# Projecting the first two tiles without the shift, in a two-layer diffusion-style block with a routed second block

## The chip, the cores and the metric

The kernel runs on one core of a Trainium2 chip. The metric is device time in microseconds (us), from three runs of the whole program. One more execution was recorded by the hardware profiler; every row below is from that execution.

## What is computed

The program is a chain of a two-layer block with modulation, and a second block with a recurrent group, band attention, cross attention and routed experts. Only the start of each of the two layers of the first block matters here:

```python
sc = jax.nn.silu(c)
for layer in range(DEPTH):                     # DEPTH = 2
    mod = sc @ w_mod[layer] + b_mod[layer]     # (1024) @ (1024, 6144)
    shift1, scale1, gate1, shift2, scale2, gate2 = [m[:, None, :] for m in jnp.split(mod, 6, axis=-1)]
    h = rmsnorm(x, g_attn[layer]) * (1.0 + scale1) + shift1
    o = mixer_layer(h, w_in[layer], ...)       # begins with proj = h @ w_in
    ...
```

x is 512 tokens of 1024 features, w_in is 1024 by 3078, and everything is float32. The second block also needs `softplus(-lam)` of 512 numbers, far behind.

## The kernel before

**Layout.** Features lie on partitions, so x is eight pieces `xT[:, k, :]` of 128 by 512. A projection tile is 128 output features by 512 tokens. Its precision is kept by splitting both factors into a rounded part and a rest: per k three matmuls, `w_hi*h_hi`, `w_hi*h_lo` and `w_lo*h_hi` (lines 689 to 691), 24 in a tile. ScalarE makes the rounded part of a block of weights (two tiles wide, `proj_split`, L1424) and VectorE the rest (`proj_rest`, L1921); in the same way `h_hi` (`hT_r`, L1351) is made by ScalarE out of `hn`, and `h_lo` by VectorE.

**The start.** SyncE's queue loads small rows, constants, x (2 MB), two small tensors (`forget_bias_t`, `diff_lambda`), then the first 2048 columns of w_mod, which are shift1 and scale1, in eight blocks of 1 MB (`load_first`, L416), with the first two blocks of w_in (1 MB each) after the sixth and after the eighth. TensorE turns x (L628), sums its squares over the partitions (L662), multiplies silu(c) with the eight blocks (`mod_products`, L639: four column groups of 32, a 128x512 float32 matmul in each), and turns the sums into columns (`mod_fold`, L646). VectorE adds them to `pc` (L2003), forms the gain, and `norm` makes `hn = x * gain * rs` and the rest; ScalarE adds the shift as it rounds. While the w_mod blocks arrive, VectorE also does a log-sigmoid of 128x4 numbers for the second block (L1795 to L1858) and the reciprocal of the norm's root (L1861).

**The layer loop** runs twice (`Fori`). Tiles 0 and 1 are projected as a pair, k by k, as the pieces of h arrive (`proj_pair`, banks 0 and 1); tiles 2, 3, ... follow one by one in banks 0 and 1 in turn, each after the copy out of the bank (`acc_copied`). The rotary step of tile r has one fp32 matmul of its own for r < 4 (L891), issued behind tile r+1; ScalarE copies a tile to one of two buffers `raw`, and the third copy waits until the first rotary step (L2072, L2075, L2082) is done (`rope_done`). Behind tile 3 come the first of 16 further mod products (one behind each tile) and the six forget columns (L896 to L898, 24 matmuls). At tile 12 VectorE does the forget gate's decay (`decay_sum`), at tile 13 the first scores of the attention begin (L813), whose row maxima VectorE takes (L2014).

## Time and profile before

| what | value |
|---|---|
| median of 3 runs | 2440.15 us (2438.64 to 2442.23) |
| profiled execution, span | 2438.2 us |
| TensorE busy | 2266.5 us (93%) |
| VectorE busy | 1207.9 us (50%) |
| ScalarE busy | 857.1 us (35%) |
| mean granted TensorE clock | 0.982 |

The span of the profiled execution is 2.0 us under the median of the runs. A row of the timeline gives the start, the duration, the engine and line, output<-input with its shape, and in brackets the idle time of the engine before it and what ended that. PEld is the load of weights, PE the matmul; PE rows overlap because their ends are modelled, so the time from start to start is what one costs.

### The profile page before, as it was taken

The page shows a single profiled execution, that of the slowest core. Times are in us where ns is not written, and L with a number is a line of the kernel's source. Part 1 is how long each engine was busy: PE and PEld are TensorE (multiplying, and loading weights), DVE is VectorE, ACT ScalarE, POOL GpSimd, SP SyncE. Part 2 cuts the span into 40 slices and gives each one's busy share as a digit, 9 for nine tenths or more (in the row PEclk, how much of TensorE's full clock was granted, in tenths as well). Part 3 has the DMA queues.
Part 4 walks back from the last instruction along what each step waited for, and adds up shares of the span by engine and source line. Part 5 has one row for each costly group of instructions (what it writes and reads, how often), then busy time and mean ns, then how long its engine had stood idle before and what let it go on. Part 6 is the DMA issues. An engine that isn't in the chain of part 4 may idle for free.

```text
span 2438.2 us, 31772 instructions
## 1 busy us (share of the span) xinstructions
PE 2266.5 (93%) x11324; PEld 1547.7 (63%) x11324; DVE 1207.9 (50%) x2321; ACT 857.1 (35%) x1565; POOL 80.9 (3%) x84
## 2 busy tenths in 40 slices
PE   6999899999999998999999999989989899887887
PEld 3667567888886766678888867758856333333332
DVE  6574736525525856665445455766243332323234
ACT  3234634323323254633223245464342222212123
POOL 0000000000000000000000000000000211111110
PEclk9999999999999999999999999999999999999999
DMA  7762063323333741043233322203315699999996
GB/s 272 208 201 70 8 213 98 102 80 104 104 79 100 214 137 36 19 121 87 95 104 97 110 71 86 79 27 121 121 44 240 268 390 387 422 398 399 412 400 275
DMA packets 214550, 414.34 MB, mean 170 GB/s; under 512 B 20951, under 2 KB 177249, under 8 KB 197857
## 3 DMA queue, kind: packets, MB, share of 16 engines
q1 hardware_dynamic: 200833, 398.68, 46.0%
q0 software_dynamic: 11520, 8.43, 1.1%
q10 hardware_dynamic: 2016, 4.81, 0.5%
q8 instruction: 115, 1.88, 0.3%
q14 instruction: 66, 0.54, 0.1%
HBM read 420.24 MB, written 25.17 MB: 183 GB/s over the span
## 4 chain that ended last, share of the span: by engine, by line
PE 72%; DMA 9%; DVE 8%; issue 5%; ACT 4%; SPq 1%; ACTq 0%; DVEq 0%; PEldq 0%; PEld 0%; POOLq 0%
PE bank L765 10%; PE bank L766 9%; PE bank L767 9%; DMA arena<-in_expert_up_w 8%; PE bank L689 7%; PE bank L691 6%; PE bank L690 6%; PE bank L1190 5%; PE bank L1191 2%; PE bank L1199 2%; PE bank L813 2%; PE bank L790 2%; DVE tmp L1789 1%; PE bank L639 1%; PE bank L803 1%
## 5 line engine op out<-in xcount | busy, mean ns | idle before, releaser
L1190 PE MATMUL bank<-arena,xT 128*64 128x512 f32 x560 | 265.6, 631 | 49.9 <-DMA arena<-in_expert_up_w 37.8
L689 PE MATMUL bank<-hT_r,arena_r 128*128 128x512 f32 x704 | 286.2, 407 | 10.4 <-DVE arena_r L1980 3.0
L691 PE MATMUL bank<-hT_r,arena_r 128*128 128x512 f32 x704 | 275.4, 391 | 0.0
L767 PE MATMUL bank<-hT_r,arena_r 128*128 128x512 f32 x704 | 274.0, 389 | 0.0
L1191 PE MATMUL bank<-arena,xT 128*64 128x512 f32 x560 | 266.0, 632 | 0.0
L690 PE MATMUL bank<-arena_r 128*128 128x512 f32 x656 | 256.3, 391 | 0.0
L2410 DVE TENSOR_TENSOR hT<-hT,bank 64x512 f32<-64x512 f32 x80 | 54.9, 686 | 316.8 <-PE bank L1178 220.2
L766 PE MATMUL bank<-arena_r,S_r 128*128 128x512 f32 x528 | 205.5, 389 | 0.0
L1190 PEld LDWEIGHTS bank<-arena,xT 128*64 128x64 f32 x560 | 79.1, 145 | 172.0 <-issue 155.6
L689 PEld LDWEIGHTS bank<-hT_r,arena_r 128*128 128x128 f32 x704 | 132.4, 188 | 69.5 <-issue 20.1
L1199 PE MATMUL bank<-arena,hT 128*64 128x512 f32 x560 | 128.8, 604 | 25.6 <-ACT hT L1731 25.2
L691 PEld LDWEIGHTS bank<-hT_r,arena_r 128*128 128x128 f32 x704 | 132.4, 188 | 28.8
L767 PEld LDWEIGHTS bank<-hT_r,arena_r 128*128 128x128 f32 x704 | 132.1, 188 | 27.5
L690 PEld LDWEIGHTS bank<-arena_r 128*128 128x128 f32 x656 | 123.7, 189 | 25.5 <-issue 2.2
L765 PE MATMUL bank<-hT_r,S_r 128*128 128x512 f32 x352 | 138.1, 392 | 1.7 <-DVE arena_r L1789 1.7
L1727 ACT ACTIVATE hT<-bank 64x512 f32<-64x512 f32 x80 | 47.2, 591 | 262.7 <-PE bank L1191 261.8
L767 PE MATMUL bank<-arena_r 128*128 128x512 f32 x352 | 136.9, 389 | 0.0
L2129 DVE TENSOR_SCALAR tmp<-gpad,pc 128x512 f32<-128x512 f32 x44 | 24.1, 547 | 182.1 <-ACT gpad L1530 182.1
L766 PEld LDWEIGHTS bank<-arena_r,S_r 128*128 128x128 f32 x528 | 99.1, 188 | 20.0
L1934 DVE TENSOR_TENSOR arena_r<-arena,S_r 128x1024 fp32r<-128x1024 f32 x66 | 78.0, 1221 | 66.3 <-ACT S_r L1411 66.3
L1191 PEld LDWEIGHTS bank<-arena,xT 128*64 128x64 f32 x560 | 79.1, 145 | 43.8 <-issue 43.8
L766 PE MATMUL bank<-arena_r,tmp_r 128*128 128x512 f32 x272 | 105.8, 389 | 0.0
(449 smaller groups left out, 4336.4 us busy)
## 6 DMA issues: line engine op xcount, KB each, us to landing
arena<-in_expert_gate_w SPq DMA_DIRECT2D x32, 2048.0 KB, 14.8
arena<-in_expert_up_w SPq DMA_DIRECT2D x32, 2048.0 KB, 20.1
arena<-in_expert_down_w SPq DMA_DIRECT2D x32, 2048.0 KB, 20.4
arena<-in_w_up SPq DMA_DIRECT2D x88, 512.0 KB, 5.0
arena<-in_w_in SPq DMA_DIRECT2D x68, 512.0 KB, 6.0
arena<-in_w_mod SPq DMA_DIRECT2D x32, 1024.0 KB, 6.8
arena<-in_w_down SPq DMA_DIRECT2D x40, 512.0 KB, 4.0
S<-in_w_mod SPq DMA_DIRECT2D x16, 1024.0 KB, 4.9
```

Of the source, the lines that this page charges most:

```text
L689: mm(b[:, :], w_h, hT_r[:, k, :], start=start, stop=False)
L690: mm(b[:, :], w_h, lo, start=False, stop=False)
L691: return mm(b[:, :], w_l, hT_r[:, k, :], start=False, stop=stop)
L765: mm(b[:, :], w_h, hi, start=start, stop=False)
L766: mm(b[:, :], w_h, lo, start=False, stop=False)
L767: return mm(b[:, :], w_slot(arena_r, i, piece)[:, at:at + P], hi, start=False, stop=stop)
L790: ins = nc.tensor.transpose(bank[4 + tile % 2][:, kb * P:(kb + 1) * P], probs(u)[:, kb * P:(kb + 1) * P], ident)
L1190: mm(bank[half][gate0:gate0 + SUB, :], x, expert_weights(slot, 0)[:, k, :], start=k == 0, stop=k == KD - 1)
L1191: ins = mm(bank[half][up0:up0 + SUB, :], x, expert_weights(slot, 1)[:, k, :], start=k == 0, stop=k == KD - 1)
L1199: ins = mm(bank[2 + half][c * SUB:(c + 1) * SUB, :], x, expert_weights(slot, 2)[:, k, c * T:(c + 1) * T], start=k == 0, stop=k == 3)
L1934: vec.tensor_tensor(w_slot(arena_r, i, piece), w_slot(arena, i, piece), w_hi[i % 2][piece], ALU.subtract).then_inc(s["lo_ready"], 1)
L2410: tt(ea[at, :], eg[at, :], bank[half][at, :], ALU.mult).then_inc(s["act_e"], 1)
```

## The change

w_mod's first block is cut in half: the scale half of each of the eight blocks (0.5 MB each) is loaded first, right behind x and the first block of w_in, and the shift half after it. The two small tensors move to ScalarE's queue. The first two tiles are projected from `hn` without the shift, ahead of the loop (`first_pair`); the eight shift products stand between the pair's steps k = 2 to 5, then 32 small matmuls (two columns wide) multiply the same weights with the shift, and the result goes as a bias into the two copies. Then the loop makes h again, with the shift. Tiles 2 and 3 become a pair (banks 6 and 7) in both layers. In the sum of squares VectorE adds six of the eight pieces, so that TensorE has three matmuls for it and not eight. The log-sigmoid goes from the start into the loop's first pass, behind tile 11 on VectorE. Seven matmuls on constants are added while x arrives.

```diff
+            load_in(0, 0, w_in)
+            for k in (0, 1, 2, 3, 4, 5, 7):
+                load_scale(k)
+            sp.wait_ge(s["rows_turned"], 4)
+            load_scale(6)
             for k in range(KD):
-                if k == FIRST_IN:
-                    load_in(0, 0, w_in)
-                load_first(k)
+                load_shift(k)
             load_in(0, 1, w_in)
...
-            norm(0)
             pe.wait_ge(s["silu_c"], 1)
-            pe.wait_ge(s["x_updated"], KD)
             for k in range(KD):
-                pe.wait_ge(s[f"mod_in{k}"], 16)
-                mod_products(bank[0], first_w[:, k, :, :], k)
-            mod_fold(1, toep[:, 0, :], bank[6])
+                if k == 6:
+                    norm_summed(0)
+                pe.wait_ge(s[f"mod_in{4 + k // 2}"], 32)
+                first_products(bank[0], first_w[k][:, 2:4, :], k)
+            first_fold(1, toep[:, 0, :], KD)
             keep_busy(bank[5], 3, QUARTER)
+            def first_pair():
+                pe.wait_ge(s["lo_ready"], 2)
+                for k in range(KD):
+                    pe.wait_ge(s["h_ready"], k + 1)
+                    pe.wait_ge(s["h_lo_ready"], k + 1)
+                    for j in range(2):
+                        ins = proj_mm(bank[j], 0, k, j, normed_lo(k), k == 0, k == KD - 1)
+                        if k == KD - 1 and j == 0:
+                            ins.then_inc(s["tiles_done"], 1)
+                    if 2 <= k < 6:
+                        for n in (2 * k - 4, 2 * k - 3):
+                            pe.wait_ge(s[f"mod_in{n // 2}"], 32)
+                            first_products(bank[3], first_w[n][:, 0:2, :], n)
+                    if k == 6:
+                        first_fold(2, toep[:, 1, :], 0)
+                pe.wait_ge(s["shift_split"], 1)
+                for j in range(2):
+                    for k in range(KD):
+                        at = (k % 4) * QUARTER + j * P
+                        for part, w in enumerate((proj_hi(0, k // 4), proj_lo(arena_r, 0, k // 4))):
+                            ins = mm(bank[6][:, 2 * KD + 2 * j:2 * KD + 2 * j + 2], w[:, at:at + P], shift_parts[:, k, :], start=k == 0 and part == 0, stop=k == KD - 1 and part == 1)
+                ins.then_inc(s["tiles_done"], 1)
...
                         if h == 0:
-                            proj_pair(i, normed_lo, arrived)
-                        elif h >= 2:
+                            with pe.If(l > 0):
+                                proj_pair(i, normed_lo, arrived)
+                        elif h == 1:
+                            pe.wait_ge(s["lo_ready"], pieces(l, 2))
+                            pe.wait_ge(s["bias_ready"], 1)
+                            proj_pair(1, normed_lo, arrived, 6)
+                        elif h >= 4:
...
+            proj_rest(0, 1)
+            dve.wait_ge(s["tiles_done"], TILES + 2)
+            link(vec.tensor_reduce(first_bias[:, :], bank[6][:, 2 * KD:2 * KD + 4].rearrange("p (j m) -> p j m", j=2), AX.X, ALU.add))
+            vec.tensor_scalar(first_bias[:, :], first_bias[:, :], -(HD // 2) ** -0.5, None, ALU.mult).then_inc(s["bias_ready"], 1)
...
+                    if h == TERMS_AT + 1:
+                        with dve.If(l < 1):
+                            log_sigmoid_terms(pc2[:, E_LAM:E_LAM + CT], ..., link_terms)
+                            log_sigmoid_sum(pc2[:, E_LAM:E_LAM + CT], ..., link_terms)
```

SyncE's queue at the start, before (first fence) and in the changed kernel (second). `in_w_mod` 128x2048 is a whole block, 128x1024 a half; `in_w_in` x2 is one block of the projection's weights.

```order
L405 DMA hT<-in_x 128x4x1024
L406 DMA fb<-in_forget_bias_t 6x2
L407 DMA lamp<-in_diff_lambda 128x256
L416 DMA arena<-in_w_mod 128x2048 x6
L449 DMA arena<-in_w_in 128x4x256 x2
L416 DMA arena<-in_w_mod 128x2048 x2
L449 DMA arena<-in_w_in 128x4x256 x2
```

```order
L410 DMA hT<-in_x 128x4x1024
L456 DMA arena<-in_w_in 128x4x256 x2
L419 DMA arena<-in_w_mod 128x1024 x7
L419 DMA S<-in_w_mod 128x1024
L423 DMA arena<-in_w_mod 128x1024 x6
L423 DMA S<-in_w_mod 128x1024
L423 DMA arena<-in_w_mod 128x1024
L456 DMA arena<-in_w_in 128x4x256 x2
```

The first block of w_in now stands ahead of all of w_mod, and the scale halves ahead of the shift halves.

VectorE at tile 11 of the loop, before (first) and in the changed kernel (second). `rs<-rs,std 6x512` is the first step of the decay sum, `arena_r<-arena,arena_r` the rest of a block of weights.

```order
L2082 TENSOR_TENSOR arena<-tmp 128x512
L1920 REGISTER_ALU
L1921 TENSOR_TENSOR arena_r<-arena,arena_r 128x1024
L1920 REGISTER_ALU
L1921 TENSOR_TENSOR arena_r<-arena,arena_r 128x1024
L2029 ISA
L2030 TENSOR_TENSOR pc<-pc,bank 128x16
```

```order
L2191 TENSOR_TENSOR arena<-tmp 128x512
L2199 COMPARE_AND_BRANCH
L1882 TENSOR_SCALAR small<-small 128x4
L1883 RECIPROCAL small<-small 128x4
L1884 TENSOR_TENSOR small<-small 128x4
L1885 TENSOR_TENSOR small<-small 128x4
L1886 TENSOR_SCALAR small<-small 128x4
L1869 SCALAR_TENSOR_TENSOR small<-small 128x4 x7
L1893 TENSOR_SCALAR small<-pc 128x4
L1869 SCALAR_TENSOR_TENSOR small<-small 128x4
L2203 TENSOR_SCALAR pc<-small 128x4
L2204 TENSOR_SCALAR pc<-small 128x4
```

The log-sigmoid now stands between the last rotary step and the rest of block 7, ahead of the decay sum.

TensorE at the end of the pair in the changed kernel (the small matmuls are new and have no counterpart before):

```order
L873 MATMUL bank<-kc,toep 128x4
L704 MATMUL bank<-hT_r,arena_r 128x512 [waits h_lo_ready,h_ready]
L705 MATMUL bank<-arena_r 128x512
L706 MATMUL bank<-hT_r,arena_r 128x512
L704 MATMUL bank<-hT_r,arena_r 128x512
L705 MATMUL bank<-arena_r 128x512
L706 MATMUL bank<-hT_r,arena_r 128x512
L906 MATMUL bank<-shift_parts,arena_r 128x2 [waits shift_split]
L906 MATMUL bank<-shift_parts,arena_r 128x2 x31
```

The 32 small matmuls stand behind the last step of the pair and wait for the shift.

## Rows read from the trace of the kernel before

**Rows 1.** The page: busy time and share of the span.
```profile
PE 2266.5 (93%) x11324; PEld 1547.7 (63%) x11324; DVE 1207.9 (50%) x2321; ACT 857.1 (35%) x1565; POOL 80.9 (3%) x84
```

**Rows 2.** Timeline of the start: start us, us, engine, line, what.
```profile
11.53 7.28 PE L628 MATMUL bank<-kc,hT 128*128 128x128 f32 x32 [4.50 <-DMA hT<-in_x]
...
18.64 7.60 PE L662 MATMUL bank<-tmp,kc 128*128 128x512 f32 x16
...
26.16 5.36 PE L639 MATMUL bank<-arena,rt 128*32 128x512 f32 x48
...
26.37 0.69 ACT L1345 ACTIVATE std<-bank,epsc 128x512 f32<-128x512 f32 x1
...
33.49 3.35 DVE L1861 RECIPROCAL rs<-std 128x512 f32<-128x512 f32 x1
35.31 2.00 ACT L1424 ACTIVATE arena_r<-arena 128x1024 fp32r<-128x1024 f32 x2 [5.06 <-DMA arena<-in_w_in]
...
42.68 1.06 PE L646 MATMUL bank<-kc,toep 128*128 128x4 f32 x8 [0.73 <-ACT toep L1456]
...
44.67 1.42 DVE L1789 SCALAR_TENSOR_TENSOR tmp<-xT,pc,rs 128x512 f32<-128x512 f32 x2
...
47.11 0.47 PE L689 MATMUL bank<-hT_r,arena_r 128*128 128x512 f32 x1 [1.97 <-DVE arena_r L1789]
```

**Rows 3.** Windows of the same stretch: length, busy (count) by engine, clock, DMA, GB/s.
```profile
5.00:6.00 1.00, 0.00 (x0) 0.00 (x0) 0.00 (x0) 0.00 (x0) 0.00 (x0) 1.00 1.03 412
...
10.40:12.00 1.60, 0.47 (x2) 0.48 (x3) 0.00 (x0) 0.00 (x0) 0.00 (x0) 1.00 0.24 88
12.30:26.90 14.60, 14.53 (x54) 7.42 (x56) 7.29 (x19) 6.85 (x10) 0.00 (x0) 1.00 1.01 426
27.00:31.50 4.50, 4.50 (x44) 1.17 (x36) 2.11 (x14) 1.85 (x5) 0.00 (x0) 1.00 1.05 253
```

**Rows 4.** Windows by stage, same columns: the clock.
```profile
31.50:37.80 6.30, 0.02 (x4) 0.00 (x0) 5.99 (x13) 2.00 (x2) 0.00 (x0) 0.75 1.02 402
...
45.20:47.10 1.90, 0.00 (x0) 0.03 (x1) 1.67 (x4) 1.38 (x2) 0.00 (x0) 1.00 1.08 281
47.10:59.80 12.70, 12.69 (x48) 9.89 (x48) 11.72 (x17) 6.97 (x10) 0.00 (x0) 0.87 0.10 20
```

**Rows 5.** Timeline from the pair's end to the forget columns, first layer.
```profile
59.85 1.13 PE L891 MATMUL bank<-tmp,kc 128*128 128x512 f32 x2
...
61.01 0.69 DVE L2075 TENSOR_TENSOR tmp<-bank,kc 128x512 f32<-128x512 f32 x1 [0.19 <-PE bank L891]
...
73.72 1.12 PE L891 MATMUL bank<-tmp,kc 128*128 128x512 f32 x2
...
74.28 0.79 PE L896 MATMUL bank<-hT_r,wfz_r 128*6 128x512 f32 x1
```

**Rows 6.** Timeline: two matmuls of 256 columns in a row (tile 4).
```profile
82.39 0.28 PE L720 MATMUL bank<-arena_r,hT_r 128*128 128x256 f32 x1
82.51 0.28 PE L721 MATMUL bank<-arena_r 128*128 128x256 f32 x1
```

**Rows 7.** Timeline: the log-sigmoid's first and last instruction on VectorE.
```profile
30.28 0.17 DVE L1795 TENSOR_SCALAR small<-small 128x4 f32<-128x4 f32 x1 [0.27 <-ACT small L1453]
...
33.14 0.16 DVE L1858 TENSOR_SCALAR pc<-small 128x4 f32<-128x4 f32 x1
```

**Rows 8.** VectorE's timeline, tiles 11 to 13 of the first layer.
```profile
134.70 0.69 DVE L2072 TENSOR_TENSOR tmp<-tmp,kc 128x512 f32<-128x512 f32 x1 [2.44 <-ACT tmp L1479]
...
151.01 0.28 DVE L2014 CUSTOM_DVE_ANT_0 tmp<-bank,kc 128x128 f32<-128x128 f32 x1
```

**Rows 9.** Waits of TensorE's weight loads, 140 to 155 us.
```profile
PEld bank L813 <- DVE mx L2014: 2.2, 1, 2.2
```

**Rows 10.** Timeline, second layer: tile 2 begins, third rotary matmul.
```profile
761.87 0.80 PE L689 MATMUL bank<-hT_r,arena_r 128*128 128x512 f32 x1
...
775.17 1.13 PE L891 MATMUL bank<-tmp,kc 128*128 128x512 f32 x2
```

More of the change, by code:

```diff
@@ L1472, in _ @@
                     act.wait_ge(s["tiles_done"], tiles(l, h + 1))
[L1473 removed]
+                    b = bank[4 + h if h in (2, 3) else h % 2]
                     if h in ROPE:
@@ L1492, in _ @@
                         af(z6[0], bank[4][0:C_HEADS, :], ACT.Identity, bias=pc[0:C_HEADS, 106:107]).then_inc(s["z_ready"], 1)
+                    if h == TERMS_AT:
+                        with act.If(l < 1):
+                            act.wait_ge(s["lam2"], 1)
+                            af(small[:, 40:44], small[:, 40:44], ACT.Exp, scale=-1.0).then_inc(s["lam2"], 1)
                     if h == FZ_AT + 2:
@@ L1870, in sum_square @@
                     vec.tensor_tensor(rs[:, :], rs[:, :], sq[:, k % 2, :], ALU.add).then_inc(s["sq_used"], 1)
+            for k in range(KD):
+                dve.wait_ge(s["x_turned"], k + 1)
+                vec.tensor_copy(xT[:, k, :], bank[(4, 5, 1, 2)[k % 4]][:, :]).then_inc(s["x_updated"], 1)
+                if 1 <= k <= SUMMED:
+                    sum_square(0, k - 1)
+            dve.wait_ge(s["lam_exp"], 1)
+            for l in range(DEPTH):
+                lam_init = 0.8 - 0.6 * math.exp(-0.3 * l)
+                link(vec.tensor_tensor(small[:, 28:29], small[:, 21 + 2 * l:22 + 2 * l], small[:, 20 + 2 * l:21 + 2 * l], ALU.subtract))
+                link(vec.tensor_scalar(pcall[:, l, C_LAM:C_LAM + 1], small[:, 28:29], -lam_init, None, ALU.add))
+                link(vec.tensor_scalar(pcall[:, l, C_SUB:C_SUB + 1], pcall[:, l, C_SUB:C_SUB + 1], 1.0 - lam_init, None, ALU.mult))
+            link(vec.tensor_copy(pc[:, :], pcall[:, 0, :]))
             def norm_recip(n):
```

237 lines of the change are left out of this document (146 added, 91 removed).

## The prediction

> **What bounds the kernel now.** I read the page first: TensorE is busy 93% of the span [rows 1]. So over most of the program a microsecond counts only if TensorE waits for it; elsewhere it is hidden. Then the timeline of the start, because the change works there [rows 2]. TensorE runs from 11.5 to 31.5 us, idles 6.3 us until the seventh block of w_mod lands. The windows say why: the DMA engines are full all along, from 12.3 on [rows 3, 4]. So the start is bound by bytes: 8 MB of w_mod and 1 MB of w_in between x and the gain. From the last product a chain of small steps (fold at 42.68, first hn at 44.67) leads to the first projection matmul at 47.11 [rows 2]. That pair takes 12.7 us, paced by VectorE and ScalarE, and the forget columns begin at 74.28 [rows 4, 5]. I take 74.28 as the mark: behind it the program is the same up to tile 11, so what the mark moves, the end moves. Last I looked for places later in the loop where TensorE waits for VectorE, since the log-sigmoid goes there.
>
> **Part 1, the start of the first pair.** The gain now needs 1 MB of w_in and 4 MB of scale. x stops flowing at 10.4 us; then the engines are nearly idle to 12.3, where the two small tensors stand in the queue (88 GB/s) [rows 3]. These leave the queue, so I let w_in begin at 10.4. In its 1 KB packets w_in moved at 253 GB/s [rows 3]: 1.05 MB in 4.1, to 14.5. Before TensorE may sum the squares it wants six scale halves, 3.15 MB, in 4 KB packets like x, at about 404 GB/s (412 in a window of x): 7.8, to 22.3. Landing is later than flowing: 1.1 us for x (10.4 to 11.5), 3.8 for w_in (31.5 to 35.31) [rows 2, 3]; I take 1.7, nearer x since the packets are like x's: 24.0. Then two products (5.36/6 us a block of 512 columns, half of that each: 0.9) and three norm matmuls (7.60/8 each: 2.9). TensorE's clock fell to its lower level, 1.2 GHz, within the idle 6.3 us (mean 0.75), and again within the pair (mean 0.87), behind only 1.9 idle us [rows 4]. The pair's mean makes 12.7 x 0.13 x 2 = 3.3 us at half speed, a cost of 1.7. From 18.8 to 24 TensorE will be busy about a third of the time, so I expect the lower level here too, at the same 1.7. So 29.5; root 0.7 + 0.1; the reciprocal 3.35, which other work hid before and nothing hides now; 0.9 from the fold's end to the first hn (43.74 to 44.67); 2.44 from there to the first matmul [rows 2]. The pair starts at **37.0**, against 47.1: **10.1 saved**. Ends: 32.7 (w_in at 426 GB/s, 1.1 landing, clock up) and 40.8 (3.8 landing and twice the clock's price).
>
> The Trainium skill (DMA: Bandwidth & Descriptors, Specifications) puts the smallest transfer for line rate at 512 B, by which the 1 KB packets of w_in would run as fast as the blocks of w_mod. The trace disagrees, 253 against 426 GB/s [rows 3]; by the rule w_in would take 2.5 us and the start be 1.6 us earlier.
>
> **Part 2, the first pair.** Before it took 12.7 us, 48 matmuls at about 0.227 apart (10.9) with the clock low for part of it [rows 4]. Now TensorE also does eight shift products of 0.45 and a fold of 0.5 in between: 10.9 + 3.6 + 0.5 = 15.0, more than the 12.3 in which VectorE delivers, so TensorE paces it. It has idled about 5 us before, so the lower clock again: 16.7. **+4.0** (+2.3 with the clock up).
>
> **Part 3, the 32 small matmuls.** None of that size is in the trace. The nearest rows are 256-column matmuls of the same type, 0.12 apart [rows 6], and the fp32 fold with 4 columns, 1.06 us for 8 (0.13) [rows 2]. With the load of 128x128 weights in each I take 0.12: **+3.8**. Ends: 2.0, if 256 columns rather than weights set the 0.12, and 6.0, if the 0.19 of a weight load is not overlapped. By the Trainium skill (TensorE: Matmul & The Clock Gate, Part 1) the sequencer spends about 62 ns on a small matmul with hardware decode off; by that alone the 32 would take an estimated 2.0 us, and no row here shows one.
>
> **Part 4, turning round.** VectorE waits for these, reduces them and scales (0.5), enters the loop past a branch (0.5, of the 0.9 of part 1), and must make hn, h_hi and h_lo again before tiles 2 and 3 can start: 2.44 [rows 2]. **+3.5**. Nothing covers it; TensorE has no other work in the queue. Ends 3.0 and 4.5.
>
> **Part 5, tiles 2 and 3, to the mark.** Before: 14.5 us from 59.8 to 74.28 for two tiles, three rotary matmuls and one mod product. Now the pair is fed by VectorE like the first was, 12.7 with a dip of the clock after the idle 3.5 us. Rotary step 0 starts behind it, since its matmul does: its result is there 1.16 later (59.85 to 61.01), then 0.69 + 0.69 + gaps, then the third copy (0.6 + 0.1), which waited in vain for a `raw` buffer until then, then rotary matmul 2, 0.56 to the mark [rows 5]: 3.9. 16.6 against 14.5: **+2.1**.
> The mark: 37.0 + 16.7 + 3.8 + 3.5 + 12.7 + 3.9 = 77.6, **3.3 us later** than 74.3.
>
> **Part 6, the log-sigmoid.** It takes 3.0 us (30.28 to 33.30, 16 small steps) and was hidden under DMA [rows 7]. Its new place is exposed: VectorE is idle 2.44 us just before tile 11's rotary step and then does 23 instructions from 134.7 to 151.0 back to back, up to the first row maximum; and TensorE waits 2.2 us for that maximum [rows 8, 9]. The added steps stand in that chain of work, so TensorE waits 5.2: **+3.0**, in the first layer only. If it hid somewhere it would be 0.
>
> **Part 7, the second layer.** Tiles 2 and 3 as a pair save the first rotary matmul ahead of tile 2, but tile 2 starts at 761.87 because its weights' rest is ready only then, so it starts no earlier. The pair ends 10.9 later, 772.7, and rotary matmul 2 can go 3.4 behind that (part 5's chain), 776.1, against 775.17 [rows 10]: **+0.9** (0 to 1.5). Branches that skip the new blocks cost nothing visible. The sum of squares, the turning of x in four banks and the small steps on `diff_lambda` lie beside the loads; at nothing, since part 1's chain begins behind them (if x's squares were late, at most 1).
>
> Sum: -10.1 + 4.0 + 3.8 + 3.5 + 2.1 + 3.0 + 0.9 = **+7.2 us**. On the profiled span that is 2445.4; carried over to the median, 2440.15 + 7.2 = **2447.3**. A measurement of this kernel can tell about 0.2% (4.9 us) from no change.
>
> **The rivals.**
> *The clock stays up (not slower).* If TensorE keeps 2.4 GHz through the sparse products, the first pair and the second, 1.7 + 1.7 + 1.4 fall away: +2.4, 2442.5, no change. For it: the added matmuls on constants, and the clock was 1.00 in all windows up to 31.5 [rows 3]. Against it: both dips before, one of them after an idle time of only 1.9 us [rows 4]. It decides only if all three places stay up; each one alone is 1.4 to 1.7.
> *The log-sigmoid is hidden.* If TensorE's wait at tile 13 is not set by VectorE's chain, part 6 is 0 and the time 2444.3, no change. For it: the chain holds block 7's weights and the decay, for which nobody waits yet. Against: they stand ahead of the maximum in the program's order, and TensorE already waits [rows 9].
> *The scale halves land late.* With the landing of w_in (3.8 and not 1.7) and an issue that holds back, the start is 2 to 4 us later: 2450. For it: w_in's own landing [rows 2, 3]; this is also the case that the change doesn't do what it says, that scale comes hardly earlier than both did. Slower.
> *All goes well.* Start 32.7, small matmuls at 2.0 in all, the clock up: the mark is 32.7 + 15.0 + 2.0 + 3.5 + 11.3 + 3.9 = 68.4, 5.9 earlier; with +3.9 behind it the end is 2438.2, and only with the log-sigmoid hidden too, 2435.2, is it faster by over 0.2%.
>
> **How the numbers follow.** Forecast as summed 0.45; clock up 0.17; log-sigmoid hidden 0.15; late scale 0.13; all well 0.10. Slower by over 0.2%: 0.45 + 0.13 = 0.58. Within: 0.32. Faster: 0.10, the last case with whatever else I overlooked on that side. The range reaches from just under no change (2439.5, which leaves out most of the last case) to the late scale with a dear set of small matmuls (2451.5).
>
> **What would show it.** In the changed profile: the start of the first pair (37.0 against 47.1), the 32 small matmuls' length (3.8), the idle time between them and tile 2 (3.5), the forget columns' start (77.6), TensorE's wait for the first row maximum in the first layer (5.2 against 2.2 in the second), the clock in 20 to 60 us. It is wrong in size if the pair starts before 34 or after 40, and wrong in sign if the mark is before 70.

## The result, and the profile after

| kernel | median, us | ratio to before | 95% interval |
|---|---|---|---|
| before | 2440.96 (8 runs) | | |
| changed | 2454.32 (8 runs) | 1.0052 | 1.0042 to 1.0063 |

The change makes the kernel slower, by about 13 us. The forecast was 7.2 us slower, 2447.3, with a range that ended at 2451.5. So the direction was right, the size was short by some 6 us, and the measured time lies 2.8 us outside the range. The rows of the changed kernel below come from a later recording of it (e0 of the experiments, span 2452.2 us), because the one recorded first, one of the 8, ran at a low clock throughout (mean 0.84) and took 2626.4 us.

The page of the changed kernel (line 1, busy time, and TensorE's clock in 40 slices) shows the same work by the same engines as [rows 1]; TensorE is busy 15 us longer, and the clock is lower in the first slice:

```profile
span 2452.2 us, 32084 instructions
...
PE 2281.8 (93%) x11424; PEld 1559.6 (64%) x11424; DVE 1222.3 (50%) x2348; ACT 862.1 (35%) x1574; POOL 80.7 (3%) x84
...
PEclk8999999999999999999999999999999999999999
```

The timeline of its start, TensorE and what it waits for, answers to [rows 2]: norm, reciprocal, first hn, first pair (its first matmul at 36.13), the 32 small matmuls, the bias on VectorE, h made again, second pair (first matmul at 61.67), and the first forget column, which is the mark.

```profile
30.23 3.35 DVE L2081 RECIPROCAL rs<-std 128x512 f32<-128x512 f32 x1 [5.21 <-ACT std L1517]
...
33.85 1.42 DVE L1869 SCALAR_TENSOR_TENSOR tmp<-xT,pc,rs 128x512 f32<-128x512 f32 x2
...
36.13 0.52 PE L704 MATMUL bank<-hT_r,arena_r 128*128 128x512 f32 x1 [3.14 <-DVE arena_r L2090]
...
54.17 4.34 PE L906 MATMUL bank<-shift_parts,arena_r 128*128 128x2 f32 x32
58.55 0.16 DVE L2105 TENSOR_REDUCE first_bias<-bank 128x2 f32<-128x4 f32 x1 [2.87 <-PE bank L906]
...
61.67 0.76 PE L704 MATMUL bank<-hT_r,arena_r 128*128 128x512 f32 x1 [3.16 <-DVE arena_r L1869]
...
78.99 0.80 PE L953 MATMUL bank<-hT_r,wfz_r 128*6 128x512 f32 x1
```

The windows of the same stretches (after the bounds and the length: busy time of TensorE, its weight loads, VectorE, ScalarE, GpSimd; TensorE's clock; DMA share; GB/s) answer to [rows 4]. The lower level, 1.2 GHz (0.50), begins at about 57, before the small matmuls end (58.5), and lasts into the first half of the second pair:

```profile
36.10:54.20 18.10, 18.07 (x118) 12.14 (x118) 10.03 (x17) 5.96 (x9) 0.00 (x0) 0.91 0.62 209
54.20:57.00 2.80, 2.80 (x27) 2.80 (x25) 1.47 (x2) 0.00 (x0) 0.00 (x0) 0.98 1.07 146
57.00:67.00 10.00, 6.84 (x21) 5.62 (x21) 7.56 (x13) 4.87 (x7) 0.00 (x0) 0.50 0.96 266
67.00:79.00 12.00, 11.63 (x52) 7.84 (x50) 8.06 (x13) 5.92 (x9) 0.00 (x0) 0.99 0.19 73
79.00:154.00 75.00, 75.00 (x452) 55.00 (x454) 56.61 (x88) 17.34 (x24) 0.00 (x0) 1.00 0.71 211
154.00:163.00 9.00, 4.81 (x21) 3.05 (x21) 7.16 (x24) 4.03 (x11) 0.00 (x0) 0.81 0.69 234
```

The last row is the place of the log-sigmoid's cost. The waits of 140 to 170 us (engine and line, who ended the wait: total, times, longest) answer to [rows 9], where the same wait of the weight load was 2.2:

```profile
PEld bank L828 <- DVE mx L2119: 5.1, 1, 5.1
PE bank L828 <- DVE mx L2119: 4.2, 1, 4.2
```

Both rows are one wait, that of the weight load and that of the matmul behind it; the second is the time that TensorE's matmuls stand still. In the kernel before that was 1.25 us:

```profile
151.58 0.49 PE L813 MATMUL bank<-arena 32*128 32x128 f32 x4 [1.25 <-DVE mx L2014]
```

**Where the 13 us are.** I took the start of every matmul in the trace of before and in those of the experiments, lined the sequences up, and read the difference at landmarks. Minus is earlier than in the first trace of before; the numbers are us. The two last columns are kernels of the experiments below.

| place (time of before) | before again (e8) | changed (e0) | log-sigmoid back (e1) | log-sigmoid alone (e2) |
|---|---|---|---|---|
| mark, 74.3 | +0.9 | +4.7 | +4.7 | +0.8 |
| first row maximum's wait over, 151.6 | +0.9 | +7.6 | +4.7 | +3.7 |
| nine us on, 160.5 | +0.9 | +9.2 | +4.7 | +6.2 |
| end of the first attention, 280.7 | +1.1 | +11.0 | +4.7 | +6.3 |
| forget columns of layer 2, 780.1 | +0.9 | +12.1 | +5.8 | +5.9 |
| ahead of the cross attention, 1765.1 | +0.7 | +11.4 | +3.9 | +9.4 |
| behind it, 1811.1 | +0.7 | +14.5 | +7.0 | +10.7 |
| behind the first experts, 1990.7 | -2.6 | +14.9 | +7.3 | +10.1 |
| end of the experts, 2421.0 | -3.4 | +14.9 | +7.3 | +10.2 |

So in e0 about 4 to 5 us are lost at the start, 3 in the wait at tile 13, 1.6 right behind that wait, 1.8 in the first attention (where e1 loses none), 1 in layer 2 and 3 in the cross attention. The column of e8 shows how far two executions of one program lie apart: 1 us at the mark, 4 in the experts. A term below that can't be read from one trace. So the 1.8 us of the first attention say nothing of the change: e3 below, which has only tiles 2 and 3 as a pair, loses 1.9 us there in its trace, and e7 0.2.

### The profile page after: what moved, and what is told of

Same layout as the page of the kernel before. It is cut to its first block, busy times and chain, and to the rows that moved or that the text cites. A ratio compares the mean times of both kernels' runs of the same rounds, so it can differ in the third digit from the quotient of the medians.

```text
span 2624.6 us, 32084 instructions
## 1 busy us (share of the span) xinstructions
PE 2496.0 (95%) x11424; PEld 1599.0 (61%) x11424; DVE 1223.4 (47%) x2348; ACT 862.3 (33%) x1574; POOL 81.0 (3%) x84
## 4 chain that ended last, share of the span: by engine, by line
PE 82%; DVE 6%; issue 5%; ACT 4%; DMA 3%; SPq 0%; DVEq 0%; ACTq 0%; POOLq 0%
PE bank L780 10%; PE bank L781 10%; PE bank L782 10%; PE bank L704 7%; PE bank L705 6%; PE bank L706 6%; PE bank L1247 6%; PE bank L1256 5%; PE bank L1248 5%; PE bank L828 2%; DMA arena<-in_expert_up_w 2%; PE bank L805 2%; PE bank L654 1%; PE bank L818 1%; PE bank L735 1%
## 5 line engine op out<-in xcount | busy, mean ns | idle before, releaser
L1247 PE MATMUL bank<-arena,xT 128*64 128x512 f32 x560 | 295.6, 692 | 28.5 <-DVE xT L2520 18.0
L704 PE MATMUL bank<-hT_r,arena_r 128*128 128x512 f32 x704 | 303.3, 431 | 11.7 <-DVE arena_r L1869 3.2
L1248 PE MATMUL bank<-arena,xT 128*64 128x512 f32 x560 | 295.9, 692 | 0.0
L706 PE MATMUL bank<-hT_r,arena_r 128*128 128x512 f32 x704 | 294.9, 419 | 0.0
L782 PE MATMUL bank<-hT_r,arena_r 128*128 128x512 f32 x704 | 293.7, 417 | 0.0
L705 PE MATMUL bank<-arena_r 128*128 128x512 f32 x656 | 274.9, 419 | 0.0
L781 PE MATMUL bank<-arena_r,S_r 128*128 128x512 f32 x528 | 220.2, 417 | 0.0
L704 PEld LDWEIGHTS bank<-hT_r,arena_r 128*128 128x128 f32 x704 | 136.1, 193 | 86.2 <-issue 26.6
L1256 PE MATMUL bank<-arena,hT 128*64 128x512 f32 x560 | 147.9, 680 | 23.3 <-ACT hT L1811 23.1
L1247 PEld LDWEIGHTS bank<-arena,xT 128*64 128x64 f32 x560 | 82.3, 149 | 136.2 <-issue 116.0
L706 PEld LDWEIGHTS bank<-hT_r,arena_r 128*128 128x128 f32 x704 | 136.1, 193 | 40.5
L782 PEld LDWEIGHTS bank<-hT_r,arena_r 128*128 128x128 f32 x704 | 134.8, 192 | 40.8
L780 PE MATMUL bank<-hT_r,S_r 128*128 128x512 f32 x352 | 147.1, 418 | 0.5 <-DVE arena_r L1869 0.5
L782 PE MATMUL bank<-arena_r 128*128 128x512 f32 x352 | 146.8, 417 | 0.0
L1248 PEld LDWEIGHTS bank<-arena,xT 128*64 128x64 f32 x560 | 82.1, 149 | 88.0 <-issue 88.0
L1610 ACT ACTIVATE gpad<-bank 128x512 f32<-128x512 f32 x44 | 26.4, 600 | 272.7 <-PE bank L782 272.7
```

What stands on the lines that cost most here:

```text
L704: mm(b[:, :], w_h, hT_r[:, k, :], start=start, stop=False)
L705: mm(b[:, :], w_h, lo, start=False, stop=False)
L706: return mm(b[:, :], w_l, hT_r[:, k, :], start=False, stop=stop)
L780: mm(b[:, :], w_h, hi, start=start, stop=False)
L781: mm(b[:, :], w_h, lo, start=False, stop=False)
L782: return mm(b[:, :], w_slot(arena_r, i, piece)[:, at:at + P], hi, start=False, stop=stop)
```

## The experiments

Each timed kernel ran on the same chip beside before, whose medians in the four groups were 2440.99, 2440.01, 2440.32 and 2440.16. e0 to e3 are the first group, e4 to e7 the second, e8 to e11 the third, e12 to e14 the last.

**e0, the changed kernel again.**

> The changed kernel once more, for a profile that can be laid beside the one of before. Theory A (my terms hold and something behind them was left out): first pair starts near 37.0, the 32 small matmuls take 3.8 to 4.1 us, the forget columns start near 77.6 in the first layer, and over 5 us of the 13 lie behind tile 4. Theory B (the start itself was mis-sized): the forget columns start at 80 or later, and what lies behind adds 4 us or less. Time about 13 us above the kernel before in both.

Measured: 2454.69, ratio 1.0058 (1.0037 to 1.0080). It is the trace shown above.

**e1, the changed kernel with the log-sigmoid at the start again** (on VectorE ahead of the wait for the norm's root, and its exponential on ScalarE likewise).

```diff
-                    if h == TERMS_AT + 1:
-                        with dve.If(l < 1):
-                            log_sigmoid_terms(...)
-                            log_sigmoid_sum(...)
...
+            log_sigmoid_terms(...)
+            log_sigmoid_sum(...)
             dve.wait_ge(s["std_ready"], 1)
...
```

> The changed kernel with the log-sigmoid back at the start, where VectorE waits for the norm's root. If the wait for the first row maximum is extended by it one to one, 3.0 us faster than the changed kernel, about 10 us above the kernel before, and TensorE's wait for the row maximum in the first layer falls to that of the second. If VectorE's chain there has slack, 0 and the same waits.

Measured: 2447.32, 1.0021 (1.0010 to 1.0033). The wait is 2.2 again, yet the time fell by 7.4 us from e0, where the wait alone pays 2.9.

**e2, the kernel before with only the log-sigmoid moved.** The same two blocks as in e1, the other way round, in the kernel before.

> The kernel before with only the log-sigmoid moved into the loop behind tile 11. Theory of part 6: +3.0 us (5.2 us wait at the first row maximum in the first layer, 2.2 in the second). Rival: nothing, since only the first maximum is late and the later ones catch up.

Measured: 2450.38, 1.0039 (1.0027 to 1.0051), 9.4 us above before. The wait is 5.1 as in the changed kernel. So the local forecast of part 6 holds in both kernels, and in both the time moves by more. The log-sigmoid's move is the largest single loss of the change. The trace of e2 says where the next 2.5 us go: the window behind the wait has a clock of 0.69, where before has 1.00 at the same place (e2, then before). These two terms make 5.4 us. Of the rest, the cross attention takes 1.4 in this trace, and 3.5 are lost between the forget columns of layer 2 and the cross attention, where the trace has one stretch at the lower level more and a longer one (1597.8 to 1601.3, and 973 to 980 us). No trace of the changed kernel loses anything there, so whether the log-sigmoid's move brings that loss is not shown.

```profile
150.00:161.00 11.00, 6.82 (x25) 4.60 (x25) 8.77 (x25) 4.13 (x11) 0.00 (x0) 0.69 0.56 191
```

```profile
148.00:156.00 8.00, 6.75 (x42) 4.49 (x41) 6.33 (x23) 4.19 (x12) 0.00 (x0) 1.00 0.56 188
```

In e0 the matmuls behind the wait start 0.43 us apart, and from 162.6 on 0.23:

```profile
159.21 0.75 PE L828 MATMUL bank<-arena 32*128 32x128 f32 x4 [4.19 <-DVE mx L2119]
...
160.48 0.63 PE L705 MATMUL bank<-arena_r 128*128 128x512 f32 x1
160.91 0.63 PE L706 MATMUL bank<-hT_r,arena_r 128*128 128x512 f32 x1
...
162.89 0.39 PE L705 MATMUL bank<-arena_r 128*128 128x512 f32 x1
163.12 0.39 PE L706 MATMUL bank<-hT_r,arena_r 128*128 128x512 f32 x1
```

**e3, the kernel before with only tiles 2 and 3 as a pair.**

```diff
-                        elif h >= 2:
+                        elif h == 1:
+                            pe.wait_ge(s["lo_ready"], pieces(l, 2))
+                            proj_pair(1, normed_lo, lambda k: None, 6)
+                        elif h >= 4:
...
```

> The kernel before with only tiles 2 and 3 projected as a pair in banks 6 and 7, in both layers. Part 7: +0.9 us in each layer, +1.8 in all: the pair starts no earlier and the third rotary matmul comes 3.4 us behind it. Rival: a gain of about 1 us a layer, since TensorE no longer waits for a copy between tiles.

Measured: 2441.46, 1.0000 (0.9990 to 1.0011). The first forget column comes at 74.55 (before: 74.28) and in the second layer at 778.39, of which 1.8 us were there already at 760. The pair in layer 2 therefore costs 0.9, as part 7 said; so little is not seen in the time. In the first layer the pair costs nothing that can be told from scatter (from the first pair's start to the mark 27.96 us, against 27.2 to 28.1 in before, e2, e8 and e13), so the first layer's cost in the changed kernel is not the pairing itself; what differs there is that VectorE must feed it with h made again.

**e4, the wait filled with work that nobody needs.** The theory from e1 and e2: a wait of 4.2 us costs the clock too. Work in the wait should keep it.

```diff
+                        if h == EARLY_AT:
+                            with pe.If(l < 1):
+                                pe.wait_ge(s["acc_copied"], l * 24 + EARLY_AT)
+                                keep_busy(bank[0], 9)
```

> The changed kernel with nine 128x512 float32 matmuls on constants (0.43 us each, 3.8 us) put into TensorE's wait for the first row maximum, in the first layer only. Nothing else changes. Theory (the longer wait also costs the clock: in the trace of the changed kernel the granted clock is at the lower level for 3.4 us from 159.3, right behind the 5.1 us wait, and the scores and four matmuls there take twice as long): the wait for the first maximum stays (the scores start at about 159.2 again), the lower level behind it is gone, and the time falls by 1.6 us or up to 3.4. Rival (the extra loss beyond the 3 us comes from later, from how the loops line up): the time stays as it is, and the clock behind the wait does too.

Measured: 2454.64, 1.0059 (1.0046 to 1.0072), 14.6 us above the kernel before, no gain. The trace shows why it tests nothing as it stands. The nine matmuls are 18 rows of the profile, and they hold the scores up by 3.7 us:

```profile
157.06 7.99 PE L649 MATMUL bank<-one,kc 128*128 128x512 f32 x18
```

I had read the rows' spacing, 0.43 us, as the price of one matmul in the code; a float32 matmul of 512 columns stands there twice. The lower level behind the wait was gone, though, so e9 repeats it with four.

**e5, the log-sigmoid behind tile 5.** VectorE idles there (8.1 us in one piece in e0, ahead of 92.93).

```diff
-TERMS_AT = 10
+TERMS_AT = 4
```

> The changed kernel with the log-sigmoid behind tile 5 and not behind tile 11 (its exponential behind tile 4 on ScalarE), where VectorE idles for 8.1 us and then 3.0 us in the trace. The steps, the branches and the semaphores stay as they are. Theory (it is the place that costs): the wait for the first row maximum falls from 5.1 to 2.2, the clock stays up there, and the time falls by the 7.4 us that moving it back to the start gave, to about 2447.3. Rival (the branches or the 16 steps themselves cost wherever they stand in the loop): less than half of that, 2451 or more.

Measured: 2448.16, 1.0036 (1.0023 to 1.0050). That is 8.2 us above before beside it, where the changed kernel is 13.4 and 13.7 above: 5 us gained and not the 7.4 of the theory, but well over half of it. The wait is 2.2 and the clock behind it 1.00:

```profile
PEld bank L828 <- DVE mx L2119: 2.2, 1, 2.2
```

```profile
154.00:163.00 9.00, 8.03 (x41) 5.25 (x41) 6.21 (x29) 5.88 (x17) 0.00 (x0) 1.00 0.70 235
```

Steps, branches and semaphores are as in the changed kernel. What costs is the place. The rival, that they cost wherever they stand in the loop, has fallen.

**e6, 4 of the 32 small matmuls.** The shift's other products are left out here, so the bias isn't the reference's.

```diff
-                    for k in range(KD):
+                    for k in range(1):
                         at = (k % 4) * QUARTER + j * P
...
```

> The changed kernel with 4 of the 32 small matmuls (those of the first piece of h alone; the other products of the shift are left out, so the bias isn't the reference's). Theory (the small matmuls cost their own 4.3 us and also the clock: it is at its lower level for 10.2 us from 56.9, in the middle of them, and the tiles 2 and 3 begin at half speed): the second pair starts 3.8 us earlier, 57.9, the lower level is shorter or gone, and the mark (first forget column's matmul, 78.98) comes 3.8 + 3 to 5 us earlier, 71 to 72; the time falls by 7 to 9 us. Rival (the lower level comes from the idle 3.2 us while VectorE and ScalarE turn round, whatever stood ahead of them): 3.8 us earlier at the mark, 75.2, and the lower level as long as before; the time falls by 3.8.

Measured: 2456.62, 1.0071 (1.0057 to 1.0085). Both expectations missed: 28 matmuls less gained nothing; at 16.6 us above before it is, if anything, slower than the changed kernel. The trace of e6, from the small matmuls on:

```profile
54.61 2.35 DVE L1999 TENSOR_TENSOR arena_r<-arena,arena_r 128x1024 fp32r<-128x1024 f32 x2
...
55.42 0.50 PE L906 MATMUL bank<-shift_parts,arena_r 128*128 128x2 f32 x4
...
56.88 0.15 DVE L2105 TENSOR_REDUCE first_bias<-bank 128x2 f32<-128x4 f32 x1
...
59.99 0.77 PE L704 MATMUL bank<-hT_r,arena_r 128*128 128x512 f32 x1 [4.07 <-DVE arena_r L1869]
...
62.15 0.79 PE L705 MATMUL bank<-arena_r 128*128 128x512 f32 x1 [1.39 <-issue]
```

The matmuls end at 55.9, but VectorE is busy with the rest of tile 2 and 3's weights until 57.0 (2.35 us), so h is made again only from 57.6. Then TensorE gets one matmul out and stands still for 1.4 us that the profile gives to nobody ("issue"). In e0 there is no such standstill. The small matmuls had hidden VectorE's work; that they had hidden the standstill too is a guess, and its cause stays open. In e0 h is made again 5.1 us behind the first small matmul, here 2.1, so 2.9 of the 3.8 us are gained, and the standstill takes 1.4 of them back. The 1.5 that are left are not seen in the time; behind the wait for the maximum this trace loses 2.9 us to the clock and e0 1.6. The clock is low over the second pair's begin here too (0.50 from 59.3 to 66.1), with 4 small matmuls and a wait of 4.1 us; so the small ones are not needed for it.

**e7, three matmuls on constants in that wait.**

```diff
                 ins.then_inc(s["tiles_done"], 1)
+                keep_busy(bank[5], 3)
```

> The changed kernel with three 128x512 float32 matmuls on constants right behind the 32 small ones, in the 3.2 us in which TensorE waits for h to be made again (0.43 us each at the upper level, 0.85 at the lower, so 2.6 us at most: they end before the second pair can start). Theory (idle time keeps the clock down): the lower level, 10.2 us from 56.9 before, ends 3.4 us earlier or more, and the mark comes 1.7 us or more earlier, 77.3 at the latest. Rival (the small matmuls have settled it): no difference, mark at 79.0, time within 1 us of the changed kernel's.

Measured: 2453.40, 1.0054 (1.0038 to 1.0070). By the same misreading as in e4 they took 5.1 us and ended 1.2 too late. The second pair then ran with the clock up (0.99 from 63.4 to the mark, 78.6) and took 15.2 us instead of 17.3. From the first pair's start to the mark it is 40.7 us, where the six traces without filler have 41.3 to 42.9. That fits the theory that idle time keeps the clock down, but this trace alone doesn't show it: the lower stretch lasts 6.8 us here (56.8 to 63.6), as long as in e4 (61.6 to 68.4) and e5 (57.6 to 64.4), which have no filler there, and the pair escapes it mainly by starting late. Either way the filler gives about as much as it costs.

**e8, before again.**

> The kernel before once more, unchanged, for a second trace of it. The stretches at the lower clock in the attention (249.7, 266.8, 949.4, 969.9 and 1574.1 us) and in the cross attention are the question: in every changed kernel's trace so far two more stand at about 1784 and 1820 us and cost 2.0 us between 1765 and 1850, in the one trace of before none. Theory (which of the many short waits drop the clock changes from one execution to the next, whatever the kernel): this trace differs from the first of before by a us or more somewhere behind 250 us, and may show the two at 1780. Rival (the change itself brings them): the stretches stand at the same places as in the first trace, within 5 us, and there is none at 1780. Time 2440.5.

Measured: 2439.50, 1.0005 (0.9995 to 1.0014). The stretches at the lower level in the attention stand where they stood, within 1 us. In the experts two of them (at 1888 and 1908) are missing, and the trace is 3.4 us ahead at their end. Both theories were half right: the experts differ from one execution to the next, the cross attention again has none.

**e9, e4 with four matmuls.**

```diff
-                                keep_busy(bank[0], 9)
+                                keep_busy(bank[0], 4)
```

> As e4, with four matmuls on constants and not nine: each stands in the profile as two of 0.43 us, so nine took 8.0 us and held the first scores up by 3.7. Four take 3.5 us and fit into the wait of 4.2. Theory (the long wait costs the clock): no lower level between 150 and 170 us, the scores start as late as in the changed kernel (7.6 against before minus mark 4.7, so 2.9 behind), and the 1.6 to 2.9 us that the traces of the changed kernel lose behind them are gone; the time falls by about 2 from 2454.5. Rival (the filler doesn't keep the clock): the lower level stays.

Measured: 2450.04, 1.0041 (1.0027 to 1.0054), 9.7 us above before, so 3.7 to 4.0 below the changed kernel; the two intervals still overlap. The fillers take 3.7 us of the wait, the scores start as late as before the edit (2.9 us behind the mark's own shift), and the matmuls behind are 0.23 apart at once:

```profile
157.46 3.70 PE L649 MATMUL bank<-one,kc 128*128 128x512 f32 x8
161.73 0.49 PE L828 MATMUL bank<-arena 32*128 32x128 f32 x4 [0.57 <-DVE mx L2123]
...
162.49 0.39 PE L705 MATMUL bank<-arena_r 128*128 128x512 f32 x1
162.72 0.39 PE L706 MATMUL bank<-hT_r,arena_r 128*128 128x512 f32 x1
```

```profile
154.00:166.00 12.00, 11.43 (x60) 6.99 (x59) 10.11 (x29) 4.19 (x12) 0.00 (x0) 1.00 0.61 210
```

This shows the cause: the same wait, with TensorE kept busy in it, and the loss behind it is gone. In the traces it is 1.6 us (e0, e7) to 2.9 (e2: 2.5, e6: 2.9); the time fell by somewhat more than that, and with five runs the difference can't be told from scatter. That the lower level is gone rests on the traces: it is missing in both that have fillers (e4, e9) and there in all four that have the wait without them.

**e10, e5 with two matmuls in the second wait.**

> The best of the parts: the log-sigmoid behind tile 5 (e5, 2448.2) and two matmuls on constants (1.7 us at the upper level, 3.4 at the lower) in TensorE's wait for the second pass over h. With three of them (e7) the time from the first pair to the mark was 40.7 us, against 41.3 to 42.9 without, though they ended 1.2 us too late. Expected: 40 us or less from the first pair to the mark, 2446.5 in all. If the filler gives nothing, 2448.2. Neither reaches before (2440.5).

Measured: 2448.55, 1.0033 (1.0021 to 1.0045), the same as e5. From first pair to mark 41.5 us; the filler gave nothing that can be measured.

**e11, before with the two small tensors on ScalarE's queue.**

```diff
-            sp.dma_start(fb[:, :], a["forget_bias_t"])...
-            sp.dma_start(lamp[:, :, :, :], ...)...
...
+            act.dma_start(fb[:, :], a["forget_bias_t"])...
+            act.dma_start(lamp[:, :, :, :], ...)...
```

> The kernel before with one part of the change alone: the two small tensors on ScalarE's queue and not ahead of w_mod on SyncE's. Theory (the start is bound by bytes, and the engines' idle time from 10.4 to 12.3 us is made by these two): w_mod begins to flow 1.9 us earlier, the fold and the first pair start 1.9 us earlier (45.2 against 47.1), and the time falls by 1.9 to 2438.5. Rival (the idle time is the queue's own, between x and what follows it): the pair starts at 47.1 again, no difference. Second rival (the small descriptors of diff_lambda then run beside w_mod and hold it up): the pair starts later.

Measured: 2439.31, 0.9997 (0.9988 to 1.0006). The window from 10 to 12 us, 142 GB/s in e8, is full:

```profile
10.00:12.00 2.00, 0.30 (x2) 0.31 (x3) 0.00 (x0) 0.00 (x0) 0.00 (x0) 1.00 1.04 432
```

So the two small tensors did make the engines' idle time at the start of part 1: the five traces that have them in SyncE's queue (before, e8, e2, e3, e13) show 142 to 176 GB/s in that window. TensorE's wait for the seventh block of w_mod ends at 35.09, against 36.18 to 37.84 in those five. The first pair starts at 45.60. In before, e8, e2 and e3 it starts at 46.59 to 47.59, but in e13, whose start is that of before too, at 45.50, with the clock up, so the gain at the pair can't be told from scatter:

```profile
45.50 0.47 PE L689 MATMUL bank<-hT_r,arena_r 128*128 128x512 f32 x1 [1.97 <-DVE arena_r L1790]
```

In e11 the clock was low ahead of the first pair and over its first 5 us (to 50.8), and the mark (73.63) is 0.7 to 1.6 us earlier than in the four, and 0.9 later than in e13.

**e12, a delay of 0.36 us in e5; e13, one of 1.7 us in before.** Both for the cross attention. The nine traces of the changed kernel and its variants (e0, e1, e4 to e7, e9, e10, e12) show the clock at its lower level twice there and lose 3.1 us between 1765 and 1811 (my 2.0 of the expectations counted from 1777 on); e2 shows it once and loses 1.4; before, e3, e8, e11 and e14 don't show it. The code is the same, and so is the wait in it: TensorE stands still for 2.19 us for VectorE, at 1775.75 in before and at 1785.11 in e2.

```diff
             for h in range(16):
...
                 half(bank[h % 2], i + h // 2, h % 2).then_inc(s["tiles_done"], 1)
             i += 8
+            keep_busy(bank[5], 1, 216)          # e12
+            keep_busy(bank[5], 2)               # e13
```

> The kernel e5 (changed, log-sigmoid behind tile 5) with one matmul on constants of 216 columns (0.36 us) ahead of the cross attention's query projections. All changed kernels and e2 pass there without a wait for VectorE that before has (0.47 us in its row), and all of them, and none of the four traces near before, then show the clock at its lower level from about 1776 us (time of before). Theory (it is the 0.36 us in TensorE's time that decides it): with them given back, the stretches at 1781 and 1815 are gone, the 2.0 us that e5 loses against before between 1707 and 1811 become 0 to 0.4, and the time falls by 1.6, to 2446.5. Rival (something else in the change brings them): they stay, and the time rises by 0.4.

> The kernel before with two matmuls on constants of 512 columns (1.7 us in all) at the same place. Theory (a shift of TensorE's work decides which of the short waits of the cross attention drop the clock): the trace shows a lower stretch between 1776 and 1830 us that before does not have, and between 1707 and 1811 it loses more than its own 1.7 us, up to 3.7; the time rises by 1.7 to 3.7, 2442 to 2444. Rival (before never drops there): exactly 1.7 later, no lower stretch there.

Measured: e12 2448.54, 1.0036 (1.0022 to 1.0050); e13 2443.99, 1.0014 (1.0005 to 1.0022). The windows over the cross attention, of before, then of the changed kernel, then of e13:

```profile
1776.00:1812.00 36.00, 31.56 (x119) 18.49 (x118) 17.46 (x64) 15.36 (x51) 0.00 (x0) 1.00 0.00 0
```

```profile
1788.00:1826.00 38.00, 33.63 (x115) 19.40 (x114) 16.98 (x61) 14.71 (x50) 0.00 (x0) 0.92 0.00 1
```

```profile
1775.00:1813.00 38.00, 33.41 (x119) 19.22 (x120) 17.86 (x65) 15.26 (x52) 0.00 (x0) 0.96 0.00 0
```

e12 decides nothing: its delay was swallowed by a wait that follows (TensorE stood as before it at the cross attention's first score). e13's came through with 1.0 us, and with it the kernel before shows a lower stretch there and loses another 1.7 us. It is the later of the changed kernel's two alone (1808.0 to 1811.4 in e13, 1821.6 to 1825.0 in e0); behind the wait of 2.19 us itself, at 1775.14, the clock stayed at 1.00. e2 shows only the earlier one. So the kernel before can fall into the later one when its work is shifted, with no part of the change; for the earlier one that isn't shown. Which shift brings it, and why the changed kernels always have it, stays open.

**e14, a try at a better kernel:** e11 with four matmuls on constants ahead of the seventh block of w_mod.

```diff
+                if k == 6:
+                    keep_busy(bank[5], 4)
                 pe.wait_ge(s[f"mod_in{k}"], 16)
```

> A try at a kernel that beats both: before with the two small tensors on ScalarE's queue (e11: first pair 1.5 us earlier, mark 0.7 to 1.6 earlier, 2439.3) and with four matmuls on constants (3.5 us) in TensorE's idle time ahead of the seventh block of w_mod (3.66 us in e11). Theory (the clock's lower level over the first pair, 15.8 us from 33.7 in e11, comes from that idle time): it is shorter or begins later, from the pair's start to the mark 27 us or less against 28.0, and the time is 2438.0, 2.5 below before, which is at the edge of what can be told from no change. Rival (the level falls anyway behind the products): 28.0 again, 2439.3.

Measured: 2437.75, 0.9989 (0.9980 to 0.9998). The windows of e11, then of e14:

```profile
31.00:35.00 4.00, 0.44 (x5) 0.00 (x0) 3.62 (x14) 2.00 (x2) 0.00 (x0) 0.84 1.02 421
35.00:40.00 5.00, 3.87 (x16) 0.40 (x16) 3.97 (x3) 0.29 (x1) 0.00 (x0) 0.50 1.08 389
```

```profile
31.00:35.00 4.00, 4.00 (x16) 1.44 (x8) 3.59 (x15) 2.00 (x2) 0.00 (x0) 1.00 1.00 412
35.00:40.00 5.00, 2.27 (x17) 0.31 (x16) 4.05 (x3) 0.55 (x1) 0.00 (x0) 1.00 1.09 397
```

The last products run at full speed, and the pair starts 0.3 us earlier than in e11. From 40 to 51 the clock is low all the same (0.53), so over the pair's first 5 us as in e11. The kernel lies 2.4 us under before; the interval leaves out 1, but only just, and the size is below the 0.2% that I had called measurable. It is the fastest kernel of this study, and nothing of the change but the queue of the two small tensors is in it. Whether the four matmuls add anything to e11 isn't shown: the two intervals overlap.

## Why the prediction had the sign right, and where it went wrong

Six traces have the start of the changed kernel up to the mark (e0, e1, e4, e5, e9, e12), four that of before (before, e2, e8, e13). Their means, beside the steps of the forecast:

| step | forecast | measured (lowest to highest) |
|---|---|---|
| first pair starts | 37.0 | 37.3 (35.9 to 38.9) |
| first pair | 16.7 | 17.9 (16.5 to 19.3) |
| 32 small matmuls | 3.8 | 4.3 (3.6 to 4.9) |
| turning round | 3.5 | 3.3 (3.2 to 3.9) |
| tiles 2, 3 and the chain to the mark | 16.6 | 16.9 (16.2 to 17.4) |
| mark | 77.6 | 79.6 (77.7 to 81.5) |
| mark of before | 74.28 | 74.3 (72.7 to 75.2) |
| mark, later by | 3.3 | 5.3 |
| wait for the first row maximum | +3.0 | +2.9 |
| clock behind that wait | not in the sum | +1.6 to +2.9 |
| second layer, pair of tiles 2 and 3 | +0.9 | +1.0 (e3: +0.9) |
| cross attention | not in the sum | +2.7 (3.1, less a wait of 0.4 that falls away ahead of it) |

These add up to 14.0 (5.3 + 2.9 + 2.1 + 1.0 + 2.7), and 13.4 was measured (2454.3 against 2441.0). So near a fit is partly luck, since each term comes from a few traces that scatter by a us or more, and the clock's falls in the attentions and the experts, which differ from trace to trace, are left out.

**Part 1 held in its result, and partly by luck.** Some 9.5 us were saved at the first pair, 10.1 forecast (before, e2, e3, e8 and e13 start it at 46.8 on average), and that the two small tensors made the idle time behind x was confirmed by e11. But two of its terms were off and cancelled. w_in moved slower than at the 253 GB/s of its window in before: 136 GB/s from 12 to 16 us in e0. So the last two of the six scale halves landed at 25.2 and not at 24.0, and from there to the end of the norm's matmuls (29.5) it took 4.3 us and not 3.8 + 1.7.

```profile
12.00:16.00 4.00, 3.35 (x29) 2.87 (x28) 3.18 (x5) 2.32 (x6) 0.00 (x0) 1.00 1.02 136
```

```profile
25.16 1.54 PE L866 MATMUL bank<-arena,rt 128*32 128x256 f32 x16 [0.62 <-DMA arena<-in_w_mod]
26.63 1.13 PE L682 MATMUL bank<-rs,kc 128*128 128x512 f32 x2
27.59 1.88 PE L677 MATMUL bank<-tmp,kc 128*128 128x512 f32 x4
```

The two parts on which the sign of the case hung, how much is gained at the pair and how much is given back up to the mark, were both about right.

**Part 2 was mis-sized by 1.2.** The step that failed is "eight shift products of 0.45": two of them together take 1.00 us in e0, the matmul ahead of them and the one behind each take 0.1 us more, and there are four such places: 4.8 us and not 3.6. A price taken from long runs of one kind of matmul left out the change between kinds. e1 and e7 bear this out: their clock stays at 1.00 over the whole first pair, and it takes 16.5 us, where part 2 has 15.0 with the clock up.

**Part 3 was mis-sized by 0.5:** 0.12 a matmul became 0.113 at the upper level (e5: 3.63 for 32) and 0.136 in e0, where the clock falls among them. The page rule of the Trainium skill (TensorE: Matmul & The Clock Gate, Part 1), 62 ns for each with hardware decode off, would have given an estimated 2.0; the measured 3.6 to 4.9 speaks for the row, so something dearer than the sequencer set the pace here. But the 3.8 us are not what the small matmuls cost the kernel: e6 shows that under it lie 0.9 us of VectorE's work on weights and a standstill of 1.4. "VectorE waits for these" was true only because they were long.

**Part 6 is where the forecast failed.** Its own number is right to 0.1 us: 16 steps of VectorE (143.53 to 146.47, 2.9 us) came out again as 2.9 us of TensorE's wait. The mistake is the sentence "TensorE waits 5.2: +3.0", which ends at the wait. TensorE's idle time there grew from 1.25 to 4.2 us, and at 4.2 the clock fell in all four traces that had it without a filler, at 1.25 in none. I had charged the clock at three places at the start, where TensorE idles, and not at this one, where it cost 1.6 to 2.9 us. The Trainium skill says it outright (TensorE: Matmul & The Clock Gate, Why this matters for your kernels): keep gaps between bursts of matmuls short, or the clock goes back to its lower level. The traces agree, with the numbers just given, and e9 shows that it is the gap: 3.7 us of useless work in it took the loss away and left the wait.

**Part 7 held** (+1.0 against +0.9), and it is too small for the timed runs to show (e3).

**The cross attention could not have been forecast** from the trace of before, and its cause is only half known (e13). The forecast put it at nothing by the sentence "so what the mark moves, the end moves", which failed here: the same instructions behind the mark did not take the same time. It makes 2.7 of the 6.2 us by which the forecast was short, as far as traces that scatter can say; the clock behind the wait makes 2.1 and the start 2.0, which is 0.6 more than was missing.

**The rivals.** That the clock would stay up in all three of its places was wrong in every trace, and the fourth place, behind the wait for the maximum, it didn't name. It did hold in single places: the clock is 1.00 from 18 to 36 us in e5, and over the first pair in e1 and e7. That the log-sigmoid is hidden was wrong at its new place and would have been right six tiles earlier (e5). The scale halves were not late. The sign did not hang on any of the three: with the clock up or the log-sigmoid hidden the forecast's sum is still a loss (2.4 and 4.2 us).

## What to carry to other kernels

A wait that grows can cost more than it grows by: ask of each added wait on TensorE how long it is in all, and charge the clock of the matmuls behind it as well. Before small work is moved onto an engine, look for the place where that engine idles for longer than the work takes; here six tiles made a difference of 5 us (e5). And a term that can be removed is worth only what the next engine in line leaves of it: the 28 matmuls taken out in e6 were 3.8 us by their rows and gave back nothing that could be measured.

## What the runs showed of the hardware

- TensorE idle for 4.2 us, in otherwise full work, fell to 1.2 GHz for 3.4 to 6.8 us in e0, e2, e6 and e7; idle for 1.25 us at the same place it did not.
- The same wait of 2.19 us in the cross attention was followed at once by the lower level in ten traces (0.92 over 38 us in e0) and not in six (1.00 in before). A delay in the kernel before, 1.0 us of which arrived there, brought a lower stretch 33 us behind that wait (0.96 over 38 us in e13), with the clock at 1.00 in between.
- In e0 the clock fell to 0.50 at about 57 us, in the middle of the 32 matmuls of two columns (54.2 to 58.5), in which TensorE's row shows no gap. The same happened in e1, e7, e9, e10 and e12, but in e4 and e5 it fell only behind them.
- Two tiny tensors between two large transfers on one queue held the DMA engines to 142 to 176 GB/s for 2 us (five traces); with them on another queue it was 432 (e11).
- A float32 matmul of 512 columns stands in the profile as two rows that start 0.43 us apart; nine of them were x18 and took 7.99 us, at the upper level.
- Two executions of one program differ by up to 4 us in the experts' part alone, by whether the clock falls in some of its many short waits.
